# Float32 residual block on one core: three of eight chunk pairs of each up-projection tile by Strassen's scheme

## The reference, cut to what matters

```python
D_MODEL = 2048; SEQ = 256; D_FF = 5632
def swiglu(h, w_gate, w_up, w_down):
    return (jax.nn.silu(h @ w_gate) * (h @ w_up)) @ w_down
...
h = swiglu(rmsnorm(x, ffn1_pre_g[l]), ffn1_w_gate[l], ffn1_w_up[l], ffn1_w_down[l])
x = x + 0.5 * rmsnorm(h, ffn1_post_g[l])
```

## Time and profile before

| | |
|---|---|
| median of 3 runs | 1855.16 us (1854.95 to 1855.52) |
| the profiled execution's own time | 1855.51 us |
| its span, first to last instruction | 1853.7 us |
| PE busy | 1832.2 us, 99% |
| DVE busy | 932.8 us, 50% |
| ACT busy | 775.9 us, 42% |
| mean granted TensorE clock | 0.999 |

### The profile page before, as it was taken

The page is one execution under the profiler, slowest core; times in us unless marked ns, Lnnn a source line. Parts: engine busy times, 40 slices in busy tenths (PEclk is TensorE's granted clock), DMA queues, the critical chain, the costliest instruction groups (busy, mean ns, idle before and its releaser), DMA issues.

```text
span 1853.7 us, 20900 instructions
## 1 busy us (share of the span) xinstructions
PE 1832.2 (99%) x8386; PEld 1522.0 (82%) x8386; DVE 932.8 (50%) x1003; ACT 775.9 (42%) x958; POOL 49.4 (3%) x111
## 2 busy tenths in 40 slices
PE   7999999999999999999999999999999999999998
PEld 6888888888888888788888887888888888888886
DVE  5544544544544544755755557445444454444444
ACT  5434434434433433743234446343443443333432
POOL 0000000000000000260000000000000000000000
PEclk9999999999999999999999999999999999999999
DMA  6565565565565555555443655556556555656564
GB/s 227 187 198 182 189 196 181 191 194 182 193 212 186 202 185 203 184 185 178 136 136 120 213 169 195 190 183 195 188 186 197 183 182 195 211 185 201 186 200 136
DMA packets 145221, 344.79 MB, mean 186 GB/s; under 512 B 5433, under 2 KB 5505, under 8 KB 144785
## 3 DMA queue, kind: packets, MB, share of 16 engines
q1 hardware_dynamic: 144320, 339.77, 56.3%
q0 software_dynamic: 736, 4.26, 0.6%
q10 hardware_dynamic: 112, 0.03, 0.0%
HBM read 341.94 MB, written 2.10 MB: 186 GB/s over the span
## 4 chain that ended last, share of the span: by engine, by line
PE 95%; DVE 2%; DMA 2%; ACT 1%; issue 1%; SPq 0%; POOL 0%; DVEq 0%; POOLq 0%; ACTq 0%
PE ps L840 30%; PE ps L842 30%; PE ps L841 30%; PE ps L1080 1%; PE ps L975 1%; DMA raw<-in_ffn_w_gate_dram 1%; DMA raw<-in_ffn_w_down_dram 1%; DVE wlo L537 0%; DVE xT_lo L554 0%; DVE x L621 0%; PE ps L1117 0%; DMA raw<-in_ffn_w_up_dram 0%; ACT xT_hi L341 0%; DVE yg L601 0%; ACT whi L302 0%
## 5 line engine op out<-in xcount | busy, mean ns | idle before, releaser
L537 DVE TENSOR_TENSOR wlo<-raw,whi 128x1024 fp32r<-128x1024 f32 x640 | 764.3, 1224 | 876.9 <-ACT whi L302 865.1
L302 ACT ACTIVATE whi<-raw 128x1024 fp32r<-128x1024 f32 x640 | 650.3, 1054 | 1001.1 <-DMA raw<-in_ffn_w_down_dram 293.7
L840 PE MATMUL ps<-whi,xT_hi 128*128 128x512 f32 x1728 | 678.9, 393 | 6.1 <-DVE wlo L537 4.4
L842 PE MATMUL ps<-whi,xT_lo 128*128 128x512 f32 x1728 | 673.5, 390 | 0.0
L841 PE MATMUL ps<-wlo,xT_hi 128*128 128x512 f32 x1728 | 672.9, 389 | 0.0
L840 PEld LDWEIGHTS ps<-whi,xT_hi 128*128 128x128 f32 x1728 | 324.8, 188 | 73.9 <-issue 4.8
L842 PEld LDWEIGHTS ps<-whi,xT_lo 128*128 128x128 f32 x1728 | 324.6, 188 | 68.4
L841 PEld LDWEIGHTS ps<-wlo,xT_hi 128*128 128x128 f32 x1728 | 324.9, 188 | 65.7
L840 PE MATMUL ps<-whi,hT_hi 128*128 128x512 f32 x832 | 324.4, 390 | 1.5 <-DVE nat L590 1.5
L842 PE MATMUL ps<-whi,hT_lo 128*128 128x512 f32 x832 | 323.7, 389 | 0.0
L841 PE MATMUL ps<-wlo,hT_hi 128*128 128x512 f32 x832 | 323.7, 389 | 0.0
(11 more groups left out here) (102 smaller groups left out, 365.5 us busy)
## 6 DMA issues: line engine op xcount, KB each, us to landing
raw<-in_ffn_w_gate_dram SPq DMA_DIRECT2D x88, 1024.0 KB, 5.1
raw<-in_ffn_w_up_dram SPq DMA_DIRECT2D x88, 1024.0 KB, 5.1
raw<-in_ffn_w_down_dram SPq DMA_DIRECT2D x88, 1024.0 KB, 5.2
raw<-in_w_in_dram SPq DMA_DIRECT2D x40, 1024.0 KB, 5.1
raw<-in_w_out_dram SPq DMA_DIRECT2D x16, 1024.0 KB, 5.2
x<-in_x_dram SPq DMA_DIRECT2D x4, 512.0 KB, 9.2
gpost<-in_ffn_post_g_dram POOLq DMA_DIRECT2D x2, 1024.0 KB, 8.2
wp_sb<-in_w_pool_dram POOLq DMA_DIRECT2D x1, 1024.0 KB, 6.6
```

The source lines that it names most:

```text
L302: nc.scalar.activation(whi[:, g % RING, :], raw[:, g // 2 % RAW, 1024 * (g % 2):1024 * (g % 2 + 1)], ACT.Copy).then_inc(hi_ready, 1)
L537: V.tensor_tensor(wlo[:, g % RING, :], raw[:, g // 2 % RAW, 1024 * (g % 2):1024 * (g % 2 + 1)], whi[:, g % RING, :].bitcast(f32), ALU.subt ...
L840: mm(bank, a_hi, whi[:, s, c0:c0 + NT], start=start, stop=False)
L842: return mm(bank, a_lo, whi[:, s, c0:c0 + NT], start=False, stop=stop)
```

## The change

With the tokens in two groups and the chunks in pairs, two chunks of both weight matrices form a 2 x 2 block product: tokens (2) by chunks (2), times chunks (2) by matrices (2: gate, up). It is done with 8 block products of 3 matmuls. For chunk pairs 5, 6 and 7 of the tiles 1 to 10 the new code does 7 (`product`, `products`), in the form with shared sums: four sums of token blocks (`Sf`, made once in each stage by `token_sums`), four sums of weight blocks for every pair (`block_sums`, `srawA`/`srawB`), each split in hi and lo like the rest, and then 8 additions for each tile that bring the products in ps4 to ps7 into the sums in ps0 to ps3 (`combine`, `U`). Pairs 0 to 4 are done as before (`plain`). Tile 0 is as before, without looking ahead past its end.

The room for this comes from the ring: in an up stage it holds 4 halves (`slot`), from half 8 of tile 0 on, and everywhere each load is now one half, 512 KB. The gated product is kept in float32 in `hT`, and is split into `hT_hi` and `hT_lo` only in the last tile and in the down stage (`hidden_hi`, `hidden_lo`, 1024 numbers for each partition at a time), since `hT_hi` lies where the sums of weights were. The first four loads of a down stage wait for `combine` of tile 10, and the last pair of plain halves of tile 10 is loaded behind them (`last_plain`). The loops are written out for every tile.

The diff, cut to its core:

```diff
-RAW = 4
-RING = 2 * RAW
+RING = 8
...
+PAIRS = (5, 6, 7)
+PLAIN = 5
+NS = len(PAIRS)
+UP = 16 + 2 * PLAIN * (FTILES - 1)
+NQ = NS * (FTILES - 1)
...
+def slot(g):
+    for b, d in ((U1, D1), (U2, D2)):
+        if b + 8 <= g < d:
+            return (g - b) % 4
+        if b <= g < b + 8:
+            return (g - b + 4) % RING
+    return (g - (D2 if g >= D2 else D1) + 4) % RING
...
+def area(q):
+    return (q + 1) % 2
+T2, T4, T3, T1, B22, B11, B21 = range(7)
...
+                def sums(j, s):
+                    q = NS * (j - 1) + s
+                    a = area(q)
+                    if q >= 2:
+                        sp.wait_ge(p_done, 7 * (NQ * f + q - 1))
+                    elif q == 1:
+                        sp.wait_ge(sprep_ok, f + 1)
+                    sp.dma_start(sraw[a][:, T1:T1 + 2, :], part(1, PAIRS[s], j)).then_inc(s_in[a], 16)
+                    sp.dma_start(sraw[a][:, B11:B11 + 2, :], part(0, PAIRS[s], j)).then_inc(s_in[a], 16)
+                for h in range(16):
+                    if not f and h in (2, 4, 6):
+                        load_x(h // 2)
+                    load(b + h, part(h // 8, h % 8, 0))
+                    if h == 11:
+                        sums(1, 0)
...
+                plain(1, 0)
+                sums(1, 1)
+                plain(1, 1)
+                for j in range(1, FTILES):
+                    sums(j, 2)
+                    plain(j, 2)
+                    if j < FTILES - 1:
+                        sums(j + 1, 0)
+                    plain(j, 3)
+                    if j < FTILES - 1:
+                        sums(j + 1, 1)
+                        plain(j, 4)
+                        plain(j + 1, 0)
+                        plain(j + 1, 1)
...
+                    for n in range(len(order)):
+                        if b != OUT and i == 0 and n == 0:
+                            sp.wait_ge(post_ok, 8 * (FTILES - 1) * (1 if b == D1 else 2))
+                        load(b + len(order) * i + n, rows[:, order[n], 1024 * i:1024 * (i + 1)])
+                        if b != OUT and i == 0 and n == 3:
+                            last_plain(b)
+            def last_plain(d):
+                w = (w1g_d, w1u_d) if d == D1 else (w2g_d, w2u_d)
+                for m in range(2):
+                    rows = w[m][0].rearrange("(c p) f -> p c f", p=P)
+                    load(d - 2 + m, rows[:, 2 * PLAIN - 2:2 * PLAIN, (FTILES - 1) * NT:FTILES * NT])
...
+            def block_hi(f, j, s):
+                q = NS * (j - 1) + s
+                a = area(q)
+                act.wait_ge(s_in[a], 32 * (NQ // 2 * f + q // 2 + 1))
+                nc.scalar.activation(flat(shi[a][:, B22:B21 + 1, :]), flat(sraw[a][:, B22:B21 + 1, :]),
+                                     ACT.Copy).then_inc(s_hi, 1)
...
+            def hidden_hi(f, u):
+                act.wait_ge(h_ev, 2 * (FTILES * f + u + 1))
+                act.wait_ge(p_done, 7 * NQ * (f + 1))
+                act.wait_ge(post_ok, 8 * (FTILES - 1) * (f + 1))
+                nc.scalar.activation(flat(hT_hi[:, 4 * u:4 * u + 4, :]), flat(hT[:, 4 * u:4 * u + 4, :]),
+                                     ACT.Copy).then_inc(h_hi, 1)
...
+                    if h == 10:
+                        act.wait_ge(sf_ok, f + 1)
+                        nc.scalar.activation(S_hi[:].rearrange("p a b c -> p (a b c)"),
+                                             Sf[:].rearrange("p a b c -> p (a b c)"), ACT.Copy).then_inc(sfhi_ok, 1)
...
+                else:
+                    d = b + UP
+                    hi(c4)
+                    hi(c4 + 1)
+                    hi(d)
+                    hidden_hi(f, 0)
+                    hi(d + 1)
+                    hidden_hi(f, 1)
+                    hidden_out(f, j - 1)
+                    hi(d + 2)
+                    hi(d + 3)
+                    silu(b, j)
+                    hi(d + 4)
...
+            def block_sums(f, j, s):
+                q = NS * (j - 1) + s
+                a = area(q)
+                w = sraw[a]
+                dve.wait_ge(s_in[a], 32 * (NQ // 2 * f + q // 2 + 1))
+                link(V.tensor_tensor(w[:, T3:T1 + 1, :], w[:, T1:T1 + 1, :].broadcast_to([P, 2, NT]),
+                                     w[:, B22:B11 + 1, :], ALU.subtract))
+                link(V.tensor_tensor(w[:, T2, :], w[:, B22, :], w[:, T1, :], ALU.subtract))
+                V.tensor_tensor(w[:, T4, :], w[:, B21, :], w[:, T2, :], ALU.subtract).then_inc(s_t, 1)
+                dve.wait_ge(s_t, NQ * f + q + 1)
+                dve.wait_ge(s_hi, 2 * (NQ * f + q) + 1)
+                V.tensor_tensor(flat(slo[a][:, B22:B21 + 1, :]), flat(w[:, B22:B21 + 1, :]),
+                                flat(shi[a][:, B22:B21 + 1, :]).bitcast(f32), ALU.subtract).then_inc(s_lo, 1)
...
+            def token_sums(f, b):
+                dve.wait_ge(w_used, b + 4)
+                if f:
+                    dve.wait_ge(u_lo, 32)
+                else:
+                    dve.wait_ge(x_lo, 8)
+                c0 = 2 * PAIRS[0]
+                link(V.tensor_tensor(xf[:].rearrange("p n c t -> p (n c) t"), xT_hi[:, c0:KC, :].bitcast(f32),
+                                     xT_lo[:, c0:KC, :].bitcast(f32), ALU.add))
+                a11, a12, a21, a22 = (xf[:, :, c, t * P:(t + 1) * P] for t in range(TOK) for c in range(2))
+                link(V.tensor_tensor(Sf[:, 0], a21, a22, ALU.add))
+                link(V.tensor_tensor(Sf[:, 1], Sf[:, 0], a11, ALU.subtract))
+                link(V.tensor_tensor(Sf[:, 2], a21, a11, ALU.subtract))
+                V.tensor_tensor(Sf[:, 3], a12, Sf[:, 1], ALU.subtract).then_inc(sf_ok, 1)
+            def token_sums_lo(f):
+                dve.wait_ge(sfhi_ok, f + 1)
...
+            def combine(f, j):
+                pp = (FTILES - 1) * f + j - 1
+                def add(out, a, b, products, after=None):
+                    dve.wait_ge(p_done, 7 * (NQ * f + NS * j - 1) + products)
+                    if after is not None:
+                        dve.wait_ge(post_ok, 8 * pp + after)
+                    V.tensor_tensor(out[:], a[:], b[:], ALU.add).then_inc(post_ok, 1)
+                dve.wait_ge(p1_ok, pp + 1)
+                add(U[1], ps[6], U[0], 2)
+                add(ps[0], ps[0], U[0], 3)
+                add(U[2], ps[7], U[1], 4, after=1)
+                add(U[3], ps[5], U[1], 5, after=1)
+                add(ps[1], ps[1], U[2], 6, after=3)
+                add(U[0], ps[5], U[2], 6, after=3)
+                add(ps[2], ps[2], U[3], 7, after=4)
+                add(ps[3], ps[3], U[0], 7, after=6)
...
+                    if h == 8:
+                        token_sums(f, b)
+                    if h == 10:
+                        token_sums_lo(f)
...
+                gated(b, j - 1)
+                block_sums(f, j, 1)
+                sum_lo(f, j, 1)
+                plain_lo(b, j, 1)
+                block_sums(f, j, 2)
+                sum_lo(f, j, 2)
+                plain_lo(b, j, 2)
+                combine(f, j)
+                plain_lo(b, j, 3)
+                c4 = b + 16 + 2 * PLAIN * j - 2
+                if j < FTILES - 1:
+                    block_sums(f, j + 1, 0)
+                    lo(c4)
+                    sum_lo(f, j + 1, 0)
+                    lo(c4 + 1)
+                    plain_lo(b, j + 1, 0)
+                else:
...
+            def product(n, q, start):
+                a = area(q)
+                k0 = 2 * PAIRS[q % NS]
+                one, two = slice(0, P), slice(P, 2 * P)
+                bank, col, k, rows = {1: (4, B11, k0, one), 2: (0, B21, k0 + 1, one), 3: (2, B22, 3, None),
+                                      4: (1, T4, k0 + 1, two), 5: (5, T1, 0, None), 6: (6, T2, 1, None),
+                                      7: (7, T3, 2, None)}[n]
+                if rows is None:
+                    l_hi, l_lo = S_hi[:, k, q % NS, :], S_lo[:, k, q % NS, :]
+                else:
+                    l_hi, l_lo = xT_hi[:, k, rows], xT_lo[:, k, rows]
+                mm(ps[bank][:], l_hi, shi[a][:, col, :], start=start, stop=False)
+                mm(ps[bank][:], l_hi, slo[a][:, col, :], start=False, stop=False)
+                return mm(ps[bank][:], l_lo, shi[a][:, col, :], start=False, stop=q % NS == NS - 1)
+            def products(f, j, s):
+                q = NS * (j - 1) + s
+                order = (1, 6, 2, 7, 5, 4, 3) if s == NS - 1 else (1, 6, 7, 5, 2, 4, 3)
+                pe.wait_ge(s_lo, 2 * (NQ * f + q) + 2)
+                if s == 0 and j >= 2:
+                    pe.wait_ge(h_ev, 2 * (FTILES * f + j - 1))
+                for n in order:
+                    if s == 0 and n in (2, 4):
+                        pe.wait_ge(silu_ok, 2 * (FTILES * f + j - 1) + (1 if n == 2 else 2))
+                    if s == 0 and n == 3:
+                        pe.wait_ge(h_ok, 2 * (FTILES * f + j))
+                    product(n, q, s == 0).then_inc(p_done, 1)
...
+            def plain(b, j, i):
```

(102 more changed lines are left out.)

247 lines of the change are left out of this document (147 added, 100 removed).

## The result

The change made the kernel slower: 1867.24 us (median of 4 runs, 1866.25 to 1868.43) against 1855.28 us (4 runs), a ratio of 1.0066 with a 95% interval of 1.0053 to 1.0078. The prediction was 1837 us, and its range ended at 1851.

The account below looks back on a forecast made before the run. PE bounds the kernel, by matmuls times their step. From 1855.5 us, 40.8 saved, 14.2 added for the seams after tile 0 and 8.1 for those before the down stages gave 1837 us, range 1822 to 1851.

Parts of the forecast that it names:

- the part on loads: Loading and splitting a half takes 6.2 us, hidden behind PE's 8.2 us on three others, except at two seams.
- Saving by matmuls: In ten tiles of two feed-forwards, 180 of 7680 matmuls go, at 0.2267 us each: 40.8 us saved.
- Steady tile: A tile falls from 44.46 to 42.4 us, with DVE busy for 39.2 us and PE never waiting.
- the walk's slack: Following one steady tile in time order, the least margin before PE waits for DVE is 1.0 to 1.1 us.
- Operations interpolated between rows: Untimed sizes priced from measured ones: DVE 1.76 and 0.56 us, ACT 1.52 and 1.99 us.
- A load of 512 KB: Each half-size weight load lands after 3.75 us, with 2.7 and 5.1 as its ends.
- Seam after tile 0: In each feed-forward PE starts tile 1 5.9 us late, plus 1.2 for the clock: 7.1, 14.2 for both.
- Seam before the down stage: PE waits 2.0 us for plain pair 4 and 3.0 for silu; 4.05 more than before, 8.1 for both.
- DVE as the bound: DVE's queue in a steady tile limits PE, making the kernel slower; 1875 us at 3 us longer; chance 0.09.
- Small waits in steady tiles: Late loads or signals cost 0.3 to 0.8 us per tile, 6 to 16 us, so 1843 to 1853; chance 0.17.
- the seams were not shorter: The rejected rival: waits at the seams overlap or loads land sooner, half of 22.3 us, so 1826; chance 0.16.
- The clock rival: The clock drops at all four seam waits, 1.2 us also at two of 3.0: 1839.4; within the forecast's 0.55.

Follow-up runs that it names:

- x_all_first: On top of experiment 4, on ACT and DVE input column parts 5, 6 and 7 of the first feed-forward's tile 0 ahead of half 8; 1828.3 us.
- experiment 1: Changed kernel with each late input column part of the first feed-forward's tile 0 ahead of its weight half, on ACT and DVE; 1845.0 us.
- experiment 2: Changed kernel with late input column parts moved ahead of weight halves on DVE alone, ACT's order kept; 1867.7 us in a single run.
- experiment 6: Changed kernel with one edit alone: on ACT and DVE, input column parts 5, 6 and 7 of tile 0 ahead of half 8; 1840.3 us.
- experiment 8: x_all_first with the first of seven products of every pair issued twice, so PE does eight; output not the reference's; 1869.3 us.
- x_all_only: The kernel of experiment 6: the changed kernel with only the three input column parts ahead of half 8; 1840.3 us.
- Experiment 7: x_all_first with the work at the end of tile 0 (token sums, the next pair's sums and their splits) drawn forward; 1818.8 us.
- experiment 3: On top of experiment 1, the last pair of plain halves of tile 10 loaded ahead of the down stage's first four loads; 1837.1 us.
- experiment 4: On top of experiment 3, silu of tile 10 (ACT) and the gated product (DVE) ahead of the down stage's third and fourth half; 1833.7 us.
- experiment 9: x_all_first with ten linked 128x128 additions more on DVE in each of tiles 1 to 9; 1865.5 us.
- experiment 10: x_all_first with four linked 128x128 additions more on DVE in each of tiles 1 to 9; 1829.4 us.

## Why the prediction was wrong, point by point

**The step that failed** is a sentence of the part on loads: a half must be loaded and split while PE does three others, "still hidden", "except at the two seams that follow". I checked whether weights come in time in a ring of four, and they do: in x_all_first, which is free of the other waits, PE waits for no weights between the first half of tile 0 and half 15, the seam. I did not check what stands behind the wait for them. The shorter ring turned DVE's and ACT's position five halves ahead from free into a wait for PE's own progress, and the first feed-forward's tile 0 is the one place where work that PE needs at once (the input columns) is queued behind such a half. Experiments 1, 2, 5 and 6 show it: 26.9 us, where the trace has 19.9 of waits and 7.1 of clock. The sum had tile 0 of the first feed-forward, up to its seam, at nothing.

**It could have been read beforehand.** Half 8's buffer is that of half 4 by `slot`; the order on DVE has `xT_lo` behind the `wlo` of half h + 5; and the walk of the seam used "half 15 is loaded once half 11 is used" from the same table. The same rule put to half 8, in the same tile, gives PE's half 4, a load of 3.75, 1.05 and 1.22, so some 6 us, three times, about 18, where 19.9 were found.

**The rest of the sum**, with that step out, said 1837 and measured 1840.3 (experiment 6):
- *Saving by matmuls*: 40.8 said, 41.0 measured (experiment 8). Right.
- *Steady tile*: 42.4 said, 42.37 measured; DVE 39.2 said, 37.79 measured (consecutive operations overlap, which the sum did not count); the walk's slack of 1.05 measured as 1.1 to 1.2. No waits, as said. In a row of the same trace, `sloA` of the first pair of a tile runs from 186.94 to 189.23 with the tile's start at 180.75, so 8.5 after it, against 8.8 in the walk.
- *Operations interpolated between rows*: 1.76 and 0.56 on DVE as said; on ACT 1.52 and 1.99 said, 1.48 and 1.92 measured. Additions that read and write PSUM took 0.695.
- *A load of 512 KB*: 3.75 said, medians of 3.7 to 3.9 measured, but 4.7 and 4.8 for the gate parts of the Strassen buffers. The Trainium skill ("DMA: Bandwidth & Descriptors", Rules for kernel authors) asks for at least 1 MiB per DMA. Going below it cost nothing in the steady tile: the core moved 199 GB/s there and PE did not wait.
- *Seam after tile 0*: 5.9 and 1.2 for the clock said. In x_all_only the waits are 1.89 and 3.37 us in the first feed-forward, and 0.44, 2.16 and 2.70 in the second, so 5.3 in each; behind them some eight matmuls are 0.43 us apart in each, 1.6 us. Together 6.9 for the 7.1 said. The clock term is not sure: the second feed-forward of the changed kernel has 5.6 of waits there and no lower clock behind them. Experiment 7 took 9.5 from both seams.
- *Seam before the down stage*: waits of 2.0 and 3.0 said, 2.59 and 2.05 found in x_all_only in the first feed-forward, 2.95 and 0.61 in the second. The load was later than reckoned, and the wait for silu shorter. The clock, which the sum had at nothing here, came on top: between the two waits eight matmuls are 0.43 us apart in each feed-forward, 1.6 us. From the start of tile 1 to the down stage x_all_only takes 432.45 us (66.85 to 499.30) in the first, 8.4 more than ten tiles of 42.4: 4.64 are waits, 1.6 is the lower clock between them, another 1.6 is that of the seam behind tile 0, and 0.5 is not placed. Experiments 3 and 4 took 11.2 from both. Twice 1.6 is the size of the 3.3 us left, but the waits came out 1.8 shorter than said, so that match is partly luck, and how the rest is made up is not shown.

**The rivals.** DVE as the bound was wrong as a cause, though the kernel was slower: the wait was DVE's, but for its order, not for its load. Its threshold was right (experiments 9 and 10). Small waits in steady tiles did not come, and the seams were not shorter. The clock rival, with 1839.4, had the seams nearer than the forecast, as x_all_only measures them: the lower clock came in before both down stages. (The prediction places that rival inside the small-waits case; by its own numbers, 1843 to 1853, it is not.)

These are the waits of x_all_only in the first feed-forward, PE in order of time, that the last points rest on, with the first two matmuls of each stretch at the lower clock:

```profile
66.85 0.47 PE L1278 MATMUL ps<-shiB,xT_hi 128*128 128x512 f32 x1 [3.37 <-DVE sloB L718]
...
67.63 0.63 PE L1278 MATMUL ps<-shiB,S_hi 128*128 128x512 f32 x1
68.06 0.63 PE L1279 MATMUL ps<-sloB,S_hi 128*128 128x512 f32 x1
...
489.88 0.50 PE L1102 MATMUL ps<-whi,xT_hi 128*128 128x512 f32 x1 [2.59 <-DVE wlo L692]
...
490.95 0.63 PE L1103 MATMUL ps<-wlo,xT_hi 128*128 128x512 f32 x1
491.38 0.63 PE L1104 MATMUL ps<-whi,xT_lo 128*128 128x512 f32 x1
...
499.30 0.47 PE L1102 MATMUL ps<-whi,hT_hi 128*128 128x512 f32 x1 [2.05 <-issue]
```

## What to carry to other kernels

When a ring is made shorter, go through every place where an engine works ahead of its consumer and ask what stands in its queue behind the work ahead: that work now waits for the consumer, and whatever the consumer needs must stand in front of it. Do this in the first and last round of a loop above all; a steady round that is right to 0.1 us says nothing about them. And where one item is in the way in two queues, both must be mended before anything is gained.
